# Branch A's queries and keys as two more seven-product quads ahead of the heads, and TensorE's program for the heads written out

## The chip, the core and the metric

The kernel runs on one core of a Trainium2 chip. The metric is the device time of one execution in microseconds (us), the median of several runs. Engines are called TensorE (PE in the rows), VectorE (DVE), ScalarE (ACT) and SyncE (SP); PE and PEld are TensorE's matmuls and its weight loads.

## What is computed

One layer of a decoder trunk for 512 tokens of width 2048, in float32:

```python
h = _rmsnorm(x, norm_g[l])
proj = jnp.einsum('bsd,df->bsf', h, w_in[l])
aq, ak, av, az = parts[0:4]              # branch A: differential attention, 8 heads, each part 1024 wide
b_qkv = parts[4:4 + 3 * n_g]             # branch B: dilated attention, 3 groups of q, k, v, 8 heads
bz = parts[4 + 3 * n_g]
cb, cc, cx, cz = parts[5 + 3 * n_g:9 + 3 * n_g]                         # branch C: short gated convolution
gates = jax.nn.sigmoid(parts[9 + 3 * n_g] + gate_b[l])                  # 3 x 2048 wide
oa = _diff_attention(aq, ak, av, lam, slopes_a)
ya = (_rmsnorm(oa, subln_g[l]) * (1.0 - lam_init)) * jax.nn.silu(az)
x = x + (gates-weighted sum of ya, yb, yc through w_branch_a, _b, _c) @ w_out[l]
```

The change concerns `aq` and `ak`: the part of `h @ w_in` that makes branch A's queries and keys, 2 x 1024 columns.

## The kernel before

Every float32 product is made of three matmuls on operands that are split in a high part (ScalarE copies it, `w_hi`) and a low part (VectorE subtracts, `w_lo`): high times high, high times low, low times high. Weights come in units of 128 x 1024 elements (512 KB). A unit is loaded into a ring of three (`raw`), split into rings of three (`w_hi`, `w_lo`), and used by TensorE. ScalarE may split unit n+3 only when TensorE is done with unit n (`pe_used`), VectorE follows ScalarE (`hi_done`), and TensorE waits for VectorE (`lo_done`).

The program has these stages, each engine with its own list of instructions in written order:

- quad 0 (branch A's values) as plain products, 16 units;
- quads 1 to 3 (branch B's values of the three groups): a quad is 1024 columns for all 512 tokens as a 2 x 2 block product with seven products instead of eight (`quad`, 28 units, 7 x 4 x 2 x 2 x 3 = 336 matmuls of 512 columns). The result has the tokens on the partitions; VectorE scales it by the norm (`take_g`), and ScalarE's queue stores it to `c_dram`;
- the 8 heads. A head has ten blocks of 128 columns, in the order w = 0 to 9: AQ, AK, Q0, K0, Q1, K1, Q2, K2, AZ, BZ (queries and keys of A, of the three groups of B, and the gates of both). A block is 2 units, 48 matmuls of 512 columns (`multiply`), and has the channel on the partitions. VectorE scales a block out of PSUM (`scale_block`), ScalarE and VectorE split AQ, AK, Q0, K0 (`split_block`). Behind each block stand the short steps of attention: for branch A quarter q the scores (`scores_a`), `bias_a` and the maximum, the exponential (`exps_a`), `norm_a`, the transposes on TensorE (`probs_a`) and their split (`turned_a`); for branch B the same with `_b`. Branch A's scores stand at w = 2 to 5, their transposes at w = 3 to 6, its values at w = 7, its square sums (`squares_a`) at w = 8; branch B's four parts start at w = 8 and run to w = 3 of the next head;
- 24 sums of weight blocks for later stages (`sum_units`: 4 additions of 128 x 1024 on VectorE) lie among the heads. The tile `ssum` exists once: it is loaded at step t (a step is one unit), summed behind the split at t + 2, stored behind the split at t + 3, and the next load waits for that store;
- head 0 and head 7 are written out, heads 1 to 6 are a loop of two rounds of three heads, on TensorE, ScalarE and VectorE alike. Head 7 also makes the operands of the quads behind it (`combine_h`);
- quads 4 to 13 (branch C and the gates), the branch products, the output product.

In the first units of quad 4 the rest of head 7's branch B is done.

Of the kernel before, what the change touches and what calls it, by code (L numbers as in the profile page):

```python
# [28 lines left out]
P = 128  # L29
# [5 lines left out]
RING = 3  # L35
NBLK1, NHU1 = 10, 20
# [19 lines left out]


PRODUCTS, STEPS = 7, 28
UNITS_V = 16
QUADS_V, QUADS_C, QUADS_G, QUADS_O = 4, 8, 14, 2  # L60
# [29 lines left out]
SUMS_AT = {0: (5, 10), 1: (0, 5, 10, 15), 2: (0, 5, 10, 15), 3: (0, 5, 10), HEADS - 1: ()}  # L90
SUMS_BEFORE = {0: 0, 1: 2, 2: 6, 3: 10, HEADS - 1: 0}
SUMS_LOOP = 11
# [7 lines left out]
class Head:  # L100
# [4 lines left out]
    def slot(self, t):  # L105
        return (X_H + NHU1 * self.k + t) % RING

    def bank(self, w):
        return (NBLK1 * self.k + w) % RING

    def sums(self, t, at):
        if t - at not in SUMS_AT[self.k]:
            return None
        m = SUMS_BEFORE[self.k] + SUMS_AT[self.k].index(t - at)
        return m if self.j is None else SUMS_LOOP * self.j + m
# [62 lines left out]
SPLIT = [AQ, AK, Q0, K0]  # L178
# [12 lines left out]
def program(nc, wst, wg, ws, x_t, x_tok, cols_d, rows_d, lam_d, const_d, out_d):  # L191
# [8 lines left out]
    with ExitStack() as ctx:  # L200
# [21 lines left out]
        with ExitStack() as c1:  # L222
# [3 lines left out]
            s1("pad0", [P, 2048])  # L226
# [154 lines left out]
        b_saved, b_back = sem("b_saved"), sem("b_back")  # L381
        va_in, vb_in, vg_in, vh_done, vl_done = sem("va_in"), sem("vb_in"), sem("vg_in"), sem("vh_done"), sem("vl_done")
# [212 lines left out]
        def _(pe):  # L595
# [16 lines left out]
            def scaled(i, b):  # L612

                pe.wait_ge(evac_done, NBLK1 * i + (RING + b + 1))

            def split_ready(i, b):

                pe.wait_ge(ql_done, len(SPLIT) * i + (SPLIT.index(b) + 1))

            def scores_a(i, q):  # L620

                n = P * (q + 1)
                split_ready(i, AK)
# [29 lines left out]
            def squares_a(i):  # L653

                pe.wait_ge(sq_split, i + 1)
                pe.wait_ge(s_free, 9 * i + 5)
# [3 lines left out]
            def scores_b(i, c):  # L660

                scaled(i, K2)
                pe.wait_ge(s_free, 9 * i + (6 + c))
# [78 lines left out]
            def blocks(h):  # L742
                i, fresh, last = h.i, h.j is None and h.k == 0, h.j is None and h.k == HEADS - 1
                for w in range(NBLK1):
                    if fresh and w == 0:
                        pe.wait_ge(got, evicted(QUADS_V - 1, 5, 1))
                        pe.wait_ge(b_back, 32)
                    if fresh and w == 2:
                        pe.wait_ge(got, evicted(QUADS_V - 1, 6, 1))
                    pe.wait_ge(evac_done, NBLK1 * i + (w + 1))  # L750
                    pe.wait_ge(lo_done, NHU1 * i + (R_H + 2 * w + 1))
                    multiply(h.bank(w), h.slot(2 * w), act_hi, act_lo, 0, True, False)
                    if w == 8:
                        squares_a(i)
                    if last and w == 9:
                        probs_b(i, 0)
                        scores_b(i, 1)
                    pe.wait_ge(lo_done, NHU1 * i + (R_H + 2 * w + 2))
                    multiply(h.bank(w), h.slot(2 * w + 1), act_hi, act_lo, 8, False, True)
                    if w < 2 and not fresh:  # L760
                        scores_b(i - 1, 2 + w)
                    if w < 3 and not fresh:
                        probs_b(i - 1, 1 + w)
                    if w == 3 and not fresh:
                        values_b(i - 1)
                    if 2 <= w < 6:
                        scores_a(i, w - 2)
                    if 3 <= w < 7:
                        probs_a(i, w - 3)
                    if w == 7:  # L770
                        values_a(i)
                    if w == 8:
                        scores_b(i, 0)
                    if w == 9:
                        if last:
                            scores_b(i, 2)
                        else:
                            scores_b(i, 1)
                            probs_b(i, 0)
# [33 lines left out]
            def free_g(q, p):  # L813
# [3 lines left out]
                if q == QUADS_V and p in (P1, P5, P2):  # L817
                    return {P1: (evac_done, [NBLK1 * HEADS + RING] * 2), P5: (s_free, [9 * HEADS + 1] * 2),
# [11 lines left out]
            def between_g(q, p):  # L830

                def after(u):
# [3 lines left out]
                    if q == QUADS_V:  # L836
                        if n == 1:
                            scores_b(HEADS - 1, 3)
# [122 lines left out]
        def _(act):  # L961
# [45 lines left out]
            def split_1(h, t):  # L1007

                slot = h.slot(t + RING)
                act.wait_ge(raw_in[slot], 16 * h.loads(t + RING))  # L1010
                act.wait_ge(pe_used, NHU1 * h.i + (R_H + t + RING + 1))
                nc.scalar.activation(w_hi[slot][:, :], raw[slot][:, :], ACT.Copy).then_inc(hi_done, 1)  # L1012
# [34 lines left out]
            def split_block(i, w):  # L1047

                act.wait_ge(evac_done, NBLK1 * i + (RING + w + 1))
                nc.scalar.activation(qk_hi[w][:, :], blk[w][:, :], ACT.Copy).then_inc(qh_done, 1)  # L1050

            def tanh_half(i, w):
                act.wait_ge(evac_done, NBLK1 * i + (RING + w + 1))
# [24 lines left out]

            def head(h):
# [16 lines left out]
                for w in range(NBLK1):  # L1096
                    split(2 * w)
                    if last and w == 4:
                        comb_high(5, t1[0], f1, (comb_sum, 5))
                    if last and w == 7:  # L1100
                        comb_high(6, t2[0], f2, (comb_sum, 6))
                    if w in SPLIT:
                        split_block(i, w)
                    if last and w == 9:
                        turned_b(i, 0)
                    split(2 * w + 1)
                    if fresh and w == 1:
                        store_gate(QUADS_V - 1, 2)
                    if w == 3:
# [4 lines left out]
                    if w == 4:  # L1114
                        load_v(i, 1, v_b, vb_in, False)
# [3 lines left out]
                    if w == 5:  # L1119
# [3 lines left out]
                        for g in (1, 2):  # L1123
                            load_v(i, 1 + g, v_g[g], vg_in, True)
                    if w < 3 and not fresh:
                        turned_b(i - 1, 1 + w)
                    if 3 <= w < 7:
                        turned_a(i, w - 3)
                    if w == 9 and not last:
                        turned_b(i, 0)  # L1130
                    if w == 5:
                        act.wait_ge(va_in, 16 * i + 16)
                        high_v(v_a)
                    if w < 2 and not fresh:
                        exps_b(i - 1, 2 + w)
                    if 2 <= w < 6:
                        exps_a(i, w - 2)
                    if w == 7:
                        act.wait_ge(o_free, 2 * i + 2)
                        nc.scalar.activation(sq_a[:, :], o_a[:, :], ACT.Square)  # L1140
                        nc.scalar.activation(sq_hi[:, :], o_a[:, :], ACT.Square).then_inc(sq_ready, 1)
                    if w == 8:
                        act.wait_ge(s_free, 9 * i + 6)
                        nc.scalar.activation(inv_a[:, :], sq_a[:, :], ACT.Sqrt).then_inc(sd_ready, 1)
                    if w == AZ:
                        act.wait_ge(sd_ready, i + 1)
                        tanh_half(i, w)
                    if w in (8, 9):
                        exps_b(i, w - 8)
                    if w == 9:  # L1150
# [3 lines left out]
                    if w == BZ:  # L1154
                        tanh_half(i, w)
# [1101 lines left out]
```

## Time and profile before

| what | us |
|---|---|
| median of 3 runs (2529.17 to 2530.74) | 2530.38 |
| the profiled execution, its own time | 2530.92 |
| its span, first to last instruction | 2529.1 |
| TensorE busy | 2501.1 |
| VectorE busy | 1963.6 |
| ScalarE busy | 1031.8 |

Matmuls overlap in the trace: one of 512 columns is shown with 0.39 us, but the next one starts 0.23 us later, so costs on TensorE are read from starts. A group of rows with the same shape is merged into one row with its count.

### The profile page before, as it was taken

Reading aid. Unit: us, or ns where it says so; the run is one execution under the profiler, and the core shown is the slowest. Engines: PE = TensorE matmul, PEld = TensorE weight load, DVE = VectorE, ACT = ScalarE, POOL = GpSimd, SP = SyncE. Lnnn points to the kernel's source line nnn. Section 1 sums busy time; section 2 is a strip of 40 time slices with the busy share of each in tenths; the row PEclk is TensorE's granted clock in tenths of the full one; section 3 lists DMA queues with packets and bytes.
Section 4 is the critical chain, followed back from the end, with each engine's and each line's share of the span. In section 5 each row is a group of like instructions: output and inputs, shape, how many; then the busy total and the mean of one; then the engine's idle time right before and its main releaser. Section 6 shows DMA issues by size and latency. Waiting matters only on the chain.

```text
span 2529.1 us, 30668 instructions
## 1 busy us (share of the span) xinstructions
PE 2501.1 (99%) x11486; PEld 2065.3 (82%) x11486; DVE 1963.6 (78%) x2294; ACT 1031.8 (41%) x1273; POOL 0.2 (0%) x4
## 2 busy tenths in 40 slices
PE   9999999999999999999999999999999999999998
PEld 8888888888888888888887788888878887788787
DVE  8797746767676767676768887789878897898875
ACT  5343323233333233333244433344444445655644
POOL 0000000000000000000000000000000000000000
PEclk9999999999999999999999999999999999999999
DMA  8255255566665566665235545545566455787665
GB/s 315 96 193 191 78 193 196 187 237 221 237 220 204 188 237 221 237 220 204 81 111 189 211 167 191 174 158 181 186 222 202 165 174 201 275 284 243 216 229 202
DMA packets 172709, 501.98 MB, mean 198 GB/s; under 512 B 13585, under 2 KB 50706, under 8 KB 169362
## 3 DMA queue, kind: packets, MB, share of 16 engines
q1 hardware_dynamic: 88448, 338.44, 38.7%
q10 hardware_dynamic: 84114, 161.56, 18.1%
q8 instruction: 94, 1.54, 0.2%
q14 instruction: 53, 0.43, 0.1%
HBM read 407.67 MB, written 92.27 MB: 198 GB/s over the span
## 4 chain that ended last, share of the span: by engine, by line
PE 89%; DVE 5%; DMA 4%; issue 1%; ACT 1%; ACTq 0%; SPq 0%; DVEq 0%
PE proj L600 14%; PE proj L602 14%; PE proj L601 14%; PE sc_ps L600 6%; PE sc_ps L602 6%; PE sc_ps L601 6%; PE tr_ps L600 5%; PE tr_ps L602 5%; PE tr_ps L601 5%; PE o_ps L600 3%; PE o_ps L602 3%; PE o_ps L601 3%; DVE w_lo L1459 2%; DMA raw<-s_dram 1%; DMA rows<-c_dram 1%; PE tr_ps L637 1%
## 5 line engine op out<-in xcount | busy, mean ns | idle before, releaser
L600 PE MATMUL proj<-act_hi,w_hi 128*128 128x512 f32 x1280 | 505.4, 395 | 1.2 <-DVE w_lo L1503 1.2
L602 PE MATMUL proj<-act_hi,w_lo 128*128 128x512 f32 x1280 | 499.1, 390 | 0.0
L601 PE MATMUL proj<-act_lo,w_hi 128*128 128x512 f32 x1280 | 498.4, 389 | 0.0
L971 ACT ACTIVATE w_hi<-raw 128x1024 fp32r<-128x1024 f32 x280 | 296.9, 1060 | 409.6 <-PE proj L602 127.9
L1459 DVE TENSOR_TENSOR w_lo<-raw,w_hi 128x1024 fp32r<-128x1024 f32 x280 | 341.4, 1222 | 148.5 <-ACT w_hi L971 147.8
L971 ACT ACTIVATE w_hi<-kb 128x1024 fp32r<-128x1024 f32 x240 | 254.4, 1061 | 371.9 <-PE proj L602 133.6
L1459 DVE TENSOR_TENSOR w_lo<-kb,w_hi 128x1024 fp32r<-128x1024 f32 x240 | 293.3, 1223 | 96.3 <-ACT w_hi L971 95.5
L1503 DVE TENSOR_TENSOR w_lo<-raw,w_hi 128x1024 fp32r<-128x1024 f32 x160 | 195.7, 1223 | 128.3 <-ACT w_hi L1012 125.8
L602 PEld LDWEIGHTS proj<-act_hi,w_lo 128*128 128x128 f32 x1280 | 240.3, 188 | 51.1
L600 PEld LDWEIGHTS proj<-act_hi,w_hi 128*128 128x128 f32 x1280 | 240.9, 188 | 49.4 <-DVE w_lo L1503 1.4
L601 PEld LDWEIGHTS proj<-act_lo,w_hi 128*128 128x128 f32 x1280 | 240.6, 188 | 48.0
L1012 ACT ACTIVATE w_hi<-raw 128x1024 fp32r<-128x1024 f32 x160 | 168.3, 1053 | 224.3 <-PE proj L602 219.3
L1036 ACT ACTIVATE sc<-sc,nmax 128x768 f32<-128x768 f32 (+4 forms) x96 | 65.5, 682 | 225.4 <-DVE nmax L1630 126.1
L600 PE MATMUL tr_ps<-w_hi,act_hi 128*128 128x512 f32 x312 | 122.2, 392 | 5.8 <-DVE w_lo L1459 5.7
L600 PE MATMUL sc_ps<-w_hi,act_hi 128*128 128x512 f32 x320 | 125.4, 392 | 0.5 <-DVE w_lo L1459 0.5
L601 PE MATMUL sc_ps<-w_lo,act_hi 128*128 128x512 f32 x320 | 124.5, 389 | 0.0
L600 PE MATMUL sc_ps<-w_hi,tb 128*128 128x512 f32 x312 | 122.1, 391 | 0.0
L602 PE MATMUL sc_ps<-w_hi,tb 128*128 128x512 f32 x312 | 121.5, 389 | 0.0
L601 PE MATMUL sc_ps<-w_lo,tb 128*128 128x512 f32 x312 | 121.4, 389 | 0.0
L601 PE MATMUL tr_ps<-w_lo,act_hi 128*128 128x512 f32 x312 | 121.4, 389 | 0.0
L602 PE MATMUL sc_ps<-w_hi,act_lo 128*128 128x512 f32 x304 | 118.3, 389 | 0.0
L602 PE MATMUL tr_ps<-w_hi,act_lo 128*128 128x512 f32 x288 | 112.1, 389 | 0.0
(318 smaller groups left out, 4551.4 us busy)
## 6 DMA issues: line engine op xcount, KB each, us to landing
raw<-wst SPq DMA_DIRECT2D x160, 512.0 KB, 4.2
raw<-wg SPq DMA_DIRECT2D x112, 512.0 KB, 4.0
kb<-wg SPq DMA_DIRECT2D x24, 2048.0 KB, 8.0
ssum<-ws ACTq DMA_DIRECT2D x24, 2048.0 KB, 9.4
s_dram<-ssum ACTq DMA_DIRECT2D x24, 2048.0 KB, 7.7
raw<-s_dram SPq DMA_DIRECT2D x96, 512.0 KB, 4.3
raw<-ws SPq DMA_DIRECT2D x72, 512.0 KB, 4.3
kb<-wg SPq DMA_DIRECT2D x48, 512.0 KB, 6.8
```

Source lines behind the costliest of these rows:

```text
L600: nc.tensor.matmul(out, w_h, a_h, start=first, stop=False, skip_group_check=shared)
L601: nc.tensor.matmul(out, w_h, a_l, start=False, stop=False, skip_group_check=shared)
L602: return nc.tensor.matmul(out, w_l, a_h, start=False, stop=last, skip_group_check=shared)
L637: end = nc.tensor.transpose(tr_ps[idx % 2][:, n * P:(n + 1) * P], tile, ident[:, :])
L971: nc.scalar.activation(w_hi[r % RING][:, :], src, ACT.Copy).then_inc(hi_done, 1)
L1012: nc.scalar.activation(w_hi[slot][:, :], raw[slot][:, :], ACT.Copy).then_inc(hi_done, 1)
L1036: end = nc.scalar.activation(tile[:, lo:hi], tile[:, lo:hi], ACT.Exp, scale=scale, bias=nmax[:, m:m + 1], accum_out=sums[:, m:m + 1])
L1459: tt(w_lo[r % RING][:, :], src, w_hi[r % RING][:, :].bitcast(f32), ALU.subtract).then_inc(lo_done, 1)
L1503: tt(w_lo[slot][:, :], raw[slot][:, :], w_hi[slot][:, :].bitcast(f32), ALU.subtract).then_inc(lo_done, 1)
```

## The change

- `NHU1` is 16: a head has eight blocks, w = 2 to 9. Branch A's queries and keys are quads 1 and 2, ahead of branch B's values (quads 3 to 5); there are 16 quads instead of 14.
- They lie in `c_dram` with the tokens on the partitions. Per head ScalarE's queue loads the 128 columns of each (`load_qa`), TensorE turns each with four transposes into a PSUM bank (`turn_block`), in the middle of w = 2 (AQ) and w = 3 (AK); ScalarE copies the high part (`high_turn`), VectorE subtracts (`low_turn`).
- The attention steps are spread over the eight blocks: branch A's scores at w = 4 to 7, transposes at w = 5 to 8, values at w = 9, the square sums in the middle of w = 2 of the next head. Branch B runs from w = 8 to w = 5 of the next head.
- The 24 sums stand at other steps (`SUMS_FIRST`, `SUMS_LOOP`), some 4 steps apart; before they were 5 apart or more.
- In head 7 VectorE's long reciprocal (`inverse_a`) goes from w = 9 into unit 6 of the quad behind the heads, the square sums go there too (`squares_last`).
- TensorE's heads 1 to 6 are written out. ScalarE and VectorE keep their loops.

```diff
-NBLK1, NHU1 = 10, 20
+NBLK1, NHU1 = 10, 16
-QUADS_V, QUADS_C, QUADS_G, QUADS_O = 4, 8, 14, 2
+QUADS_V, QUADS_C, QUADS_G, QUADS_O = 6, 10, 16, 2
-SUMS_AT = {0: (5, 10), 1: (0, 5, 10, 15), 2: (0, 5, 10, 15), 3: (0, 5, 10), HEADS - 1: ()}
+SUMS_FIRST = (0, 4, 8, 12)
+SUMS_LOOP = (0, 5, 9, 14, 18, 23, 28, 32, 37, 41)
...
+            def turn_block(h, b):
+                i, bank = h.i, pb[h.bank(b)]
+                pe.wait_ge(qa_in[b], 16 * i + 16)
+                pe.wait_ge(evac_done, NBLK1 * i + (ENTRY[b] + 1))
+                for n in range(4):
+                    end = nc.tensor.transpose(bank[:, n * P:(n + 1) * P], qa[b][:, n, :], ident[:, :])
+                end.then_inc(a_turned, 1)
...
+                    if w == Q0:
+                        if fresh:
+                            pe.wait_ge(got, evicted(QUADS_V - 1, 6, 1))
+                        turn_block(h, AQ)
+                        if not fresh:
+                            squares_a(i - 1)
+                    if w == K0:
+                        turn_block(h, AK)
...
+                    if w < 4 and not fresh:
+                        scores_b(i - 1, w)
+                    if w < 5 and not fresh:
+                        probs_b(i - 1, w - 1)
+                    if w == 5 and not fresh:
+                        values_b(i - 1)
+                    if 4 <= w < 8:
+                        scores_a(i, w - 4)
+                    if 5 <= w < 9:
+                        probs_a(i, w - 5)
...
-            with pe.Fori(0, 2) as j:
-                for k in range(1, 4):
-                    blocks(looped(j, k))
-            blocks(fixed(HEADS - 1))
+            for n in range(1, HEADS):
+                blocks(fixed(n))
...
+            def low_turn(h, b):
+                dve.wait_ge(a_hi, 2 * h.i + (TURNED.index(b) + 1))
+                tt(qk_lo[b][:, :], pb[h.bank(b)][:, :], qk_hi[b][:, :].bitcast(f32), ALU.subtract).then_inc(evac_done, 1)
...
+                    split(t)
+                    if w == Q0:
+                        low_turn(h, AQ)
...
                     if w == 2 and not fresh:
+                        dve.wait_ge(s_ready, 9 * i - 9 + (5 + SQ_AFTER))
+                        ts(sq_a[:, :], sc_ps[0][:, :], 1.0 / P, EPS, ALU.mult, ALU.add).then_inc(s_free, 1)
...
                         if n == 3:
+                            dve.wait_ge(last_sq, 1)
+                            ts(sq_a[:, :], pb[0][:, :], 1.0 / P, EPS, ALU.mult, ALU.add).then_inc(last_read, 1)
                             turned_b(HEADS - 1, 1)
                             norm_b(HEADS - 1, 2)
-                            bias_b(HEADS - 1, 3)
+                            bias_b(HEADS - 1, 3, True)
+                        if n == 6:
+                            inverse_a(HEADS - 1)
```

Three places in VectorE's list. `ssum` rows are a sum of weight blocks, `w_lo` the split of a unit, `nmax` the maximum, `pr` the normalised probabilities that TensorE transposes.

The last quarter of branch A in the loop's first head, before (w = 5 and 6):

```order
L1503 TENSOR_TENSOR w_lo<-raw,w_hi 128x1024
L1626 SCALAR_TENSOR_TENSOR sc<-masks,slope,sc_ps 128x512 x2
...
L1630 TENSOR_SCALAR nmax<-rsum 128x2
...
L1639 SCALAR_TENSOR_TENSOR pr<-sc,rsum,tmp_a 128x512
...
L1503 TENSOR_TENSOR w_lo<-raw,w_hi 128x1024
...
L1495 TENSOR_TENSOR ssum<-ssum 128x1024
```

and now (w = 7 and 8):

```order
L1568 TENSOR_TENSOR w_lo<-raw,w_hi 128x1024
L1559 ISA
L1560 TENSOR_TENSOR ssum<-ssum 128x1024
...
L1563 TENSOR_TENSOR ssum<-ssum 128x1024
L1691 SCALAR_TENSOR_TENSOR sc<-masks,slope,sc_ps 128x512 x2
...
L1695 TENSOR_SCALAR nmax<-rsum 128x2
...
L1704 SCALAR_TENSOR_TENSOR pr<-sc,rsum,tmp_a 128x512
```

The sum stood behind the probabilities and now stands ahead of them; in the loop's first and third head.

The first block of the loop's second head, before (w = 0):

```order
L1658 TENSOR_SCALAR pr<-sc,rsum 128x768
...
L1503 TENSOR_TENSOR w_lo<-raw,w_hi 128x1024
...
L1616 TENSOR_TENSOR stage<-proj,rstd 128x512
```

and now (w = 2):

```order
L1728 TENSOR_SCALAR pr<-sc,rsum 128x768
L1567 ISA
L1568 TENSOR_TENSOR w_lo<-raw,w_hi 128x1024
L1559 ISA
L1560 TENSOR_TENSOR ssum<-ssum 128x1024
...
L1563 TENSOR_TENSOR ssum<-ssum 128x1024
L1708 ISA
L1709 TENSOR_TENSOR qk_lo<-proj,qk_hi 128x512
L1820 ISA
L1821 TENSOR_SCALAR th<-sc_ps 128x512
```

`qk_lo<-proj` is `low_turn`, and `th<-sc_ps` frees the bank that the next scores of branch B need; both stand behind a sum here.

Units 3 to 6 of the quad behind the heads, before:

```order
L1459 TENSOR_TENSOR w_lo<-raw,w_hi 128x1024
L1663 TENSOR_TENSOR pt_lo<-tr_ps,pt_hi 128x4x128
...
L1653 TENSOR_SCALAR nmax<-rsum 128x1
L1459 TENSOR_TENSOR w_lo<-raw,w_hi 128x1024
...
L1658 TENSOR_SCALAR pr<-sc,rsum 128x768
L1459 TENSOR_TENSOR w_lo<-raw,w_hi 128x1024
L1803 TENSOR_SCALAR gin<-proj,rcol 128x512 x2
```

and now:

```order
L1524 TENSOR_TENSOR w_lo<-raw,w_hi 128x1024
L2031 TENSOR_SCALAR th<-proj 128x512
L1733 TENSOR_TENSOR pt_lo<-tr_ps,pt_hi 128x4x128
...
L1723 TENSOR_SCALAR nmax<-rsum 128x1
L1524 TENSOR_TENSOR w_lo<-raw,w_hi 128x1024
...
L1728 TENSOR_SCALAR pr<-sc,rsum 128x768
L1524 TENSOR_TENSOR w_lo<-raw,w_hi 128x1024
L1771 RECIPROCAL tmp_a<-tmp_a 128x512
L1885 TENSOR_SCALAR gin<-proj,rcol 128x512 x2
```

`th<-proj` and the reciprocal have come between the splits.

## Rows read from the trace of the kernel before

**Rows 1.** The page: busy time, share of the span, instructions.

```profile
PE 2501.1 (99%) x11486; PEld 2065.3 (82%) x11486; DVE 1963.6 (78%) x2294; ACT 1031.8 (41%) x1273; POOL 0.2 (0%) x4
```

**Rows 2.** Stretches: us, busy PE, PEld, DVE, ACT, POOL (instructions), clock, DMA share, GB/s.

```profile
622.20:748.42 126.22, 126.22 (x610) 104.71 (x609) 93.60 (x136) 41.83 (x65) 0.00 (x0) 1.00 0.64 229
748.42:876.05 127.63, 126.44 (x609) 104.74 (x608) 89.09 (x132) 41.91 (x65) 0.00 (x0) 1.00 0.54 195
```

**Rows 3.** Waits, one of TensorE's: waited for, us in total, times, longest.

```profile
PE proj L600 <- DVE z_b L1616: 1.6, 1, 1.6
```

**Rows 4.** TensorE in order of time, block matmuls: start, shown duration, line, names, count.

```profile
741.84 0.39 PE L601 MATMUL proj<-act_lo,w_hi 128*128 128x512 f32 x1
...
748.19 0.39 PE L602 MATMUL proj<-act_hi,w_lo 128*128 128x512 f32 x1
```

**Rows 5.** TensorE: four transposes and the first matmul of the next block.

```profile
661.37 0.60 PE L637 MATMUL tr_ps<-ident,pr 128*128 128x128 f32 x4
661.73 0.48 PE L600 MATMUL proj<-act_hi,w_hi 128*128 128x512 f32 x1
```

**Rows 6.** VectorE in order of time: the split of a unit, a sum, what follows.

```profile
626.31 1.23 DVE L1503 TENSOR_TENSOR w_lo<-raw,w_hi 128x1024 fp32r<-128x1024 f32 x1 [1.65 <-ACT w_hi L1012]
627.45 1.22 DVE L1495 TENSOR_TENSOR ssum<-ssum 128x1024 f32<-128x1024 f32 x1
...
632.24 0.68 DVE L1674 TENSOR_TENSOR qk_lo<-stage,qk_hi 128x512 fp32r<-128x512 f32 x1
```

**Rows 7.** VectorE: branch A's last quarter, from bias to probabilities.

```profile
651.52 1.40 DVE L1626 SCALAR_TENSOR_TENSOR sc<-masks,slope,sc_ps 128x512 f32<-128x512 f32 x2
...
655.97 0.17 DVE L1636 RECIPROCAL rsum<-sums 128x2 f32<-128x2 f32 x1 [1.13 <-ACT sc L1036]
...
656.88 0.75 DVE L1639 SCALAR_TENSOR_TENSOR pr<-sc,rsum,tmp_a 128x512 f32<-128x512 f32 x1
```

**Rows 8.** TensorE: the short steps between two blocks (522.96 to 524.16, 698.05 to 699.75).

```profile
522.96 0.50 PE L629 MATMUL sc_ps<-qk_hi 64*128 64x512 f32 x2
...
524.16 0.48 PE L600 MATMUL proj<-act_hi,w_hi 128*128 128x512 f32 x1
...
698.05 0.39 PE L600 MATMUL sc_ps<-qk_hi 128*128 128x512 f32 x1
...
699.75 0.48 PE L600 MATMUL proj<-act_hi,w_hi 128*128 128x512 f32 x1
```

**Rows 9.** TensorE's end of a block, and VectorE's split of the unit it freed.

```profile
812.24 0.39 PE L600 MATMUL sc_ps<-qk_hi 128*128 128x512 f32 x1
...
813.53 1.23 DVE L1503 TENSOR_TENSOR w_lo<-raw,w_hi 128x1024 fp32r<-128x1024 f32 x1 [0.40 <-ACT w_hi L1012]
```

**Rows 10.** Branch B's bias and maximum, an exponential, and the squares' split.

```profile
701.42 0.74 DVE L1646 SCALAR_TENSOR_TENSOR sc<-masks,slope,sc_ps 128x512 f32<-128x512 f32 x1
...
703.71 0.15 DVE L1653 TENSOR_SCALAR nmax<-rsum 128x1 f32<-128x1 f32 x1
...
1323.63 0.92 ACT L1036 ACTIVATE sc<-sc,nmax 128x768 f32<-128x768 f32 x1
...
1309.62 0.69 DVE L1776 TENSOR_TENSOR sq_lo<-th,sq_hi 128x512 fp32r<-128x512 f32 x1 [1.22 <-ACT sq_hi L1141]
```

**Rows 11.** Head 7's end and the quad behind it, VectorE, TensorE and ScalarE.

```profile
1321.14 0.63 ACT L1144 ACTIVATE tmp_a<-th 128x512 f32<-128x512 f32 x1
...
1331.59 3.34 DVE L1701 RECIPROCAL tmp_a<-tmp_a 128x512 f32<-128x512 f32 x1
...
1335.81 0.47 PE L600 MATMUL proj<-w_hi,act_hi 128*128 128x512 f32 x1 [1.63 <-DVE z_b L1616]
...
1347.97 1.22 DVE L1459 TENSOR_TENSOR w_lo<-raw,w_hi 128x1024 fp32r<-128x1024 f32 x1
...
1349.29 0.47 PE L600 MATMUL sc_ps<-w_hi,tb 128*128 128x512 f32 x1
```

**Rows 12.** Transfers into and out of `ssum`, 48 of them.

```profile
DMA to landing us min/median/max: 7.4/8.8/11.3
```

More of the change, by code:

```diff
@@ L175, in gated, with step_b @@
     return 8 * q + 2 * GATED.index(d) + s + 1
-SPLIT = [AQ, AK, Q0, K0]
+SPLIT = [Q0, K0]
+TURNED = [AQ, AK]
+SQ_AFTER = 2
+def step_b(c, last):
+    return 5 + c + (not last and c >= SQ_AFTER)
 TURN_P = [4, 6, 8, 10]
@@ L743, in blocks @@
                 i, fresh, last = h.i, h.j is None and h.k == 0, h.j is None and h.k == HEADS - 1
-                for w in range(NBLK1):
-                    if fresh and w == 0:
-                        pe.wait_ge(got, evicted(QUADS_V - 1, 5, 1))
+                for w in range(Q0, NBLK1):
+                    t = 2 * (w - Q0)
+                    if fresh and w == Q0:
                         pe.wait_ge(b_back, 32)
[L748 to L752, printed above, removed]
-                    if w == 8:
[L754 to L773, printed above, removed]
@@ new lines, in blocks @@
+                    if last and w == 9:
+                        values_a(i)
+                        probs_b(i, 0)
+                        scores_b(i, 1, True)
+                    pe.wait_ge(lo_done, NHU1 * i + (R_H + t + 2))
+                    multiply(h.bank(w), h.slot(t + 1), act_hi, act_lo, 8, False, True)
+                    if w < 4 and not fresh:
[4 more added lines that the diff above has]
+                        values_b(i - 1)
@@ L1113, in head @@
                         load_v(i, 0, v_a, va_in, False)
-                    if w == 4:
-                        load_v(i, 1, v_b, vb_in, False)
+                        if not last:
+                            load_qa(i + 1)
+                    if w == 6:
+                        load_v(i, Q_V, v_b, vb_in, False)
                         if not fresh:
@@ L1123, in head @@
                         for g in (1, 2):
[L1124 to L1128, printed above, removed]
+                            load_v(i, Q_V + g, v_g[g], vg_in, True)
+                    if w < 5 and not fresh:
+                        turned_b(i - 1, w - 1)
+                    if 5 <= w < 9:
+                        turned_a(i, w - 5)
@@ L1142, in head @@
-                    if w == 8:
-                        act.wait_ge(s_free, 9 * i + 6)
-                        nc.scalar.activation(inv_a[:, :], sq_a[:, :], ACT.Sqrt).then_inc(sd_ready, 1)
+                    if w == 3 and not fresh:
+                        act.wait_ge(vb_in, 16 * i)
+                        act.wait_ge(o_ready, 2 * i - 1)
+                        high_v(v_b)
+                    if w < 4 and not fresh:
+                        exps_b(i - 1, w)
+                    if w == 3:
+                        for b in SPLIT:
+                            split_block(i, b)
@@ L1149, in head @@
                         exps_b(i, w - 8)
-                    if w == 9:
+                    if last and w == 9:
                         act.wait_ge(vb_in, 16 * i + 16)
@@ L1229, in _ @@
                     end_of(q, n)
+                    if q == QUADS_V - 1 and n == 16:
+                        for m in range(8):
+                            act.wait_ge(g_stored[m], 16 * Q_V)
+                        load_qa(0)
                     if q == QUADS_V - 1 and n == 23:
@@ L1708, in join_a, with copy_o, low_squares @@
                 stt(y_a[:, :], o_a[:, :], 0.5, blk[AZ][:, :], ALU.mult, ALU.mult).then_inc(y_ready, 1)
+            def copy_o(i):
+                dve.wait_ge(o_ready, 2 * i + 1)
+                nc.vector.tensor_copy(o_a[:, :], o_ps[:, :]).then_inc(o_free, 1)
+            def low_squares(i):
+                dve.wait_ge(sq_ready, i + 1)
+                tt(sq_lo[:, :], sq_a[:, :], sq_hi[:, :].bitcast(f32), ALU.subtract).then_inc(sq_split, 1)
             def head(h):
@@ L1722, in head @@
                 link(nc.vector.tensor_copy(slope[:, 0:1], slopes[:, bass.ds(4 * i, 1)]))
-                for w in range(NBLK1):
-                    if w < 3 and not fresh:
-                        norm_b(i - 1, 1 + w)
-                    if fresh and w == 3:
+                for w in range(Q0, NBLK1):
+                    t = 2 * (w - Q0)
+                    if w < 5 and not fresh:
+                        norm_b(i - 1, w - 1)
+                    if fresh and w == 5:
                         for n in range(8):
                             dve.wait_ge(g_stored[n], 16 * QUADS_V)
-                    if 3 <= w < 7:
-                        norm_a(i, w - 3)
+                    if 5 <= w < 9:
+                        norm_a(i, w - 5)
                     if w == 9:
                         norm_b(i, 0)
-                    split(2 * w)
+                    split(t)
+                    if w == Q0:
+                        low_turn(h, AQ)
+                    if w == K0:
+                        low_turn(h, AK)
                     if last:
```

212 lines of the change are left out of this document (119 added, 93 removed).

## The prediction

> **What bounds the kernel now.** I read the page's busy times first: TensorE is busy 2501.1 of 2529.1 us [rows 1]; some 28 us idle is all that better waiting could give, and anything else must come from fewer or shorter matmuls. Then the heads, head by head: from one head to the next TensorE takes 126.22 us and is busy throughout, at a granted clock of 1.00 (the 2.4 GHz level), while VectorE is busy 93.60 of it [rows 2]. The round that holds the loop's jump takes 127.63 us, 1.41 more. TensorE's own waits come last: near the heads there is one of note, 1.6 us at the end of head 7 [rows 3]. So the heads run at TensorE's pace, and VectorE, at 74%, is the engine that could take over.
>
> **Matmuls taken out and put in.** From 741.84 to 748.19 lie 28 steps of block matmuls, 0.2267 us each [rows 4]. Out: 8 heads x 2 blocks x 48 = 768 matmuls, 174.1 us. In: 2 quads x 336 = 672, 152.3 us. The quads in place show no gaps to speak of, and a quad's own VectorE work is the same in all of them, so I take the same pace for the two new ones. Net -21.8 us.
>
> **Transposes.** Four take 0.36 us from first start to the next block's matmul, and that matmul shows 0.48 instead of 0.39 because the switch delays it [rows 5]: 0.45 us a turn, 16 turns, 7.2 us. But the short steps now form eight groups behind blocks instead of ten, which spares two such switches a head, about 1.7 us in all. Net +5.5. The bounds: 4 (every switch hidden) and 10 (0.60 shown per group). The Trainium skill, "TensorE: Matmul & The Clock Gate", Part 4: PE-mode transpose, gives about 275 ns for one transpose in a kernel; by that the 64 would cost 17.6 us. The rows decide against it: four start within 0.36 us, so the shown duration is latency that overlaps.
>
> **The loop.** TensorE's one jump back costs 1.41 us [rows 2]; written out it goes: -1.4. VectorE's and ScalarE's loops stay, and their jumps are covered as now, since the first thing that TensorE needs of them in a head comes several us later.
>
> So far: -21.8 + 5.5 - 1.4 = -17.7 us, if nobody waits. A head then takes 105 us; VectorE loses four splits and two scalings, some 6 us, so it is busy about 87 of 105, 83%. An average doesn't tell whether TensorE waits; the places where a sum of weight blocks stands ahead of something urgent do. A split with a sum behind it holds VectorE 5.93 us (626.31 to 632.24) [rows 6], and a split starts 1.29 us after TensorE has freed the unit [rows 9].
>
> **Wait 1, the last quarter's probabilities.** In the loop's first and third head a sum stands in w = 7 between the split and `bias_a(3)`. Counted from TensorE's end of that block: split and sum done at 1.29 + 5.93 = 7.2; bias, maximum and exponential 4.45 more (651.52 to 655.97); `pr` written 1.66 after that (to 656.88 + 0.75) [rows 7]: 13.3. TensorE wants it after the scores and transposes behind w = 7 (1.20, 522.96 to 524.16) [rows 8] and one block of 48 with its switch (11.0): 12.2. It waits 1.1 to 1.2, in heads 1, 3, 4 and 6: +4.8. Now the sum stands behind `pr`, which is why no such wait exists.
>
> **Wait 2, the start of heads 2 and 5.** A sum stands behind the first split of w = 2. From TensorE's end of the first half: 1.29 + 5.93, then `low_turn` 0.6, then the scaling of the square sums 0.7 (the size of the 0.68 row) [rows 6]: 8.6. TensorE meanwhile has the turn 0.36, two square matmuls 0.6 and 24 matmuls 5.4: 6.4. It then wants the bank for `scores_b(2)`: +2.2, twice, +4.4. Behind this VectorE has slack again.
>
> **Wait 3, the squares after heads 0, 2 and 5.** Their last block has a sum behind its first half. From TensorE's end of the head, T: VectorE has split and summed at T - 5.5 + 7.2 = 1.8, then gate, scaling, split and copy (0.8 + 0.6 + 1.1 + 0.6): 4.9; bias and maximum 2.4 (701.42 to 703.71 + 0.15): 7.35; ScalarE's exponential 1.1 and two squares 1.2, VectorE's split 0.7 [rows 10]: 10.3. TensorE: values (12 matmuls, 3840 columns, 1.7 to 1.9), scores and transposes 1.70 (698.05 to 699.75) [rows 8], half a block 5.6, the turn 0.4: 9.5. +0.8 three times, +2.5. Without that sum it is 8.7 against 9.5, no wait.
>
> **The quad behind the heads.** Now TensorE starts it at 1335.81, having waited for VectorE's scaling behind the 3.34 us reciprocal; the `w_lo` for its fifth unit is ready at 1349.19, and TensorE takes it at 1349.29 [rows 11]: there is 0.1 us of slack. Added ahead of that split: `low_squares` 0.6, the square sums' scaling 0.6, and ScalarE's root (0.63) in front of the transposes' copy, 2.1 us in all, against 0.5 of new square matmuls on TensorE: a wait of 1.5. Before unit 7 the reciprocal adds its 3.4, of which some 1 us is slack left by then: 2.4. Together +3.9. In head 7 itself `inverse_a` goes, but a `comb_low` and `copy_o` come ahead of BZ's scaling: I get 1.9 us of waits there for 2.3 now, -0.4.
>
> **Sum.** -17.7 + 4.8 + 4.4 + 2.5 + 3.9 - 0.4 = -2.5 us. The profiled execution (2530.92, its span 2529.1) stands 0.5 above the median; as a difference it applies to the median alike: 2530.4 - 2.5 = 2527.9, say 2528.
>
> **Rivals.**
> (a) VectorE's slack takes it all. If waits 1 to 3 don't appear the time is -17.7 + 3.5 = -14.2: 2516; if those of the quad don't either, 2513. For it: each wait is a difference of two sums of five to eight terms, and 1 us on either side cancels most of them; the ring gives TensorE two units of margin everywhere else. Against: the terms are rows, and the order puts 4.8 us of sums ahead of each.
> (b) Slower: the one `ssum` tile. Sums 4 steps apart leave, by my count from the store at step 8 to the sum at step 11, 18.3 us for a store and a load; the median landing is 8.8 each, the largest 11.3 [rows 12]. With medians it fits by 0.7. With the largest it is 4.3 us late, and VectorE, in order, holds the split and wait 1 grows by as much in four heads: +17, 2545. It decides from 1.9 us late in each (+7.5). Against it: DMA is 64% busy now [rows 2] and hardly more later.
> (c) Slower by more of the kind I count: the same differences come out 1 us larger at nine places, 2537.
> (d) The written-out program gives nothing, because jump and fetching were not the cost: +1.4, within my range. The heads written out now, 0 and 7, show no fetch stall.
>
> **How the numbers follow.** A measurement of this kernel can tell about 0.2%, 5.1 us, from no change. My case, a total between -5 and +5, 0.50, with 2528 as the likeliest; (a), wholly or by half, 0.34; (b) and (c) 0.16. (d) lies in the first. The range takes in half of (a) and the near part of (c): 2517 to 2536; my case alone spans 2525.4 to 2535.4.
>
> **What would show it.** Head to head 105 us where nothing waits; in the loop's first and third head a wait of TensorE's transposes for `pr` of about 1.2; in heads 2 and 5 a wait of TensorE's scores for `th` of about 2; waits for `sq_lo` of about 0.8 in three heads; no gap at the former jump; in the quad behind the heads two waits for `w_lo`, 1.5 and 2.4. VectorE waiting for the load of `ssum` would be (b). If TensorE's waits between the quads and quad 6 add up to under 7 us, (a) is right. If the two new quads take other than 76.2 us each, or a turn other than 0.45, the first part is wrong.

## The result

The changed kernel takes 2536.57 us (median of 20 runs, 2532.20 to 2539.59) where the kernel before takes 2529.45 in the same comparison: 1.0026 times as long, with an interval of 1.0020 to 1.0032. A second comparison gave 1.0028 (1.0018 to 1.0039). That is 5 to 7 us slower (the medians of the two comparisons are 7.1 and 4.8 apart, the means 6.1 and 5.4), where 2.5 us faster was forecast. The time lies just outside the range. The profiled execution took 2532.20 us, with a span of 2530.4.

The page of the changed kernel, busy times, against [rows 1]: TensorE 9 us less, VectorE 74 us more.

```profile
PE 2491.8 (98%) x11454; PEld 2055.6 (81%) x11454; DVE 2037.6 (81%) x2362; ACT 1061.5 (42%) x1297; POOL 0.2 (0%) x4
```

TensorE's waits in the changed kernel (waited for, us in total, times, longest):

```profile
PE sc_ps L617 <- DVE w_lo L1524: 9.4, 8, 2.3
PE sc_ps L617 <- DVE th L1821: 4.3, 2, 2.1
PE tr_ps L659 <- DVE pr L1704: 3.8, 4, 1.0
PE sc_ps L679 <- DVE sq_lo L1786: 2.3, 3, 1.3
...
PE sc_ps L617 <- issue: 1.5, 1, 1.5
```

The three waits forecast in the heads are all there, in the number forecast: two for `th`, four for `pr`, three for `sq_lo`. The last line is the first wait of the quad behind the heads, at 1349.05: the profile names no engine that ended it. Now the stretches: the heads, then all behind them, of the changed kernel and then of the kernel before (us, busy PE, PEld, DVE, ACT, POOL, clock, DMA share, GB/s).

```profile
479.86:1333.45 853.59, 842.00 (x4107) 695.33 (x4105) 661.92 (x980) 301.55 (x479) 0.00 (x0) 1.00 0.63 218
1333.45:2530.40 1196.95, 1172.02 (x5223) 963.37 (x5223) 988.22 (x1011) 563.37 (x621) 0.00 (x0) 1.00 0.60 204
```

```profile
327.89:1335.81 1007.92, 1004.07 (x4813) 831.20 (x4811) 716.14 (x1031) 336.40 (x517) 0.00 (x0) 1.00 0.56 198
1335.81:2529.10 1193.29, 1171.15 (x5221) 963.02 (x5221) 982.79 (x1008) 558.54 (x615) 0.00 (x0) 1.00 0.60 205
```

Up to the heads the change adds 479.86 - 327.89 = 152.0 us (forecast 152.3), in the heads it takes 154.3 off, and behind them it adds 3.7. The forecast for the heads was -158.7 (-174.1 + 5.5 - 1.4 + 4.8 + 4.4 + 2.5 - 0.4). The larger part of the 4.4 that is missing there stands behind the two waits for `th`. TensorE around the first one (start, shown duration, line, names, count, idle before):

```profile
697.04 0.39 PE L619 MATMUL proj<-act_hi,w_lo 128*128 128x512 f32 x1
699.56 0.65 PE L617 MATMUL sc_ps<-qk_hi 128*128 128x512 f32 x1 [2.13 <-DVE th L1821]
700.02 0.63 PE L618 MATMUL sc_ps<-qk_lo,qk_hi 128*128 128x512 f32 x1
700.44 0.63 PE L619 MATMUL sc_ps<-qk_hi,qk_lo 128*128 128x512 f32 x1
```

and TensorE's stretches there (us, busy, granted clock, DMA share, GB/s):

```profile
690.00:696.00 6.00, 6.00 (x30) 1.00 0.22 59
696.00:700.00 4.00, 1.87 (x8) 0.96 0.32 130
700.00:704.00 4.00, 4.00 (x18) 0.61 1.04 390
704.00:710.00 6.00, 6.00 (x30) 1.00 0.37 119
```

After the wait the matmuls are 0.42 to 0.46 apart instead of 0.2267, and the granted clock is below 1.00: for some 3.4 us it is 0.50, the 1.2 GHz level. The eight us from 699.56 on lose 1.7 us by it, and the same follows the wait at 1022.76. In the profile of the kernel before the clock is below 1.00 in the last 10 us alone. The prediction has no such term.

### The profile page after: what moved, and what is told of

Its sections match the earlier page's. It is cut to its first block, busy times and chain, and to the rows that moved or that the text cites. A ratio compares the mean times of both kernels' runs of the same rounds, so it can differ in the third digit from the quotient of the medians.

```text
span 2530.4 us, 30366 instructions
## 1 busy us (share of the span) xinstructions
PE 2491.8 (98%) x11454; PEld 2055.6 (81%) x11454; DVE 2037.6 (81%) x2362; ACT 1061.5 (42%) x1297; POOL 0.2 (0%) x4
## 4 chain that ended last, share of the span: by engine, by line
PE 83%; DVE 8%; DMA 5%; issue 2%; ACT 2%; ACTq 0%; DVEq 0%; SPq 0%
PE proj L617 11%; PE proj L619 11%; PE proj L618 11%; PE tr_ps L617 6%; PE tr_ps L619 6%; PE tr_ps L618 6%; PE sc_ps L617 6%; PE sc_ps L618 6%; PE sc_ps L619 6%; PE o_ps L618 3%; PE o_ps L619 3%; PE o_ps L617 3%; DVE w_lo L1524 2%; DMA rows<-c_dram 1%; PE tr_ps L659 1%
## 5 line engine op out<-in xcount | busy, mean ns | idle before, releaser
L1003 ACT ACTIVATE w_hi<-kb 128x1024 fp32r<-128x1024 f32 x280 | 297.3, 1062 | 436.2 <-PE proj L619 154.4
L1524 DVE TENSOR_TENSOR w_lo<-kb,w_hi 128x1024 fp32r<-128x1024 f32 x280 | 342.9, 1225 | 116.8 <-ACT w_hi L1003 116.2
L617 PE MATMUL proj<-act_hi,w_hi 128*128 128x512 f32 x1024 | 406.4, 397 | 0.0
L619 PE MATMUL proj<-act_hi,w_lo 128*128 128x512 f32 x1024 | 399.7, 390 | 0.0
L618 PE MATMUL proj<-act_lo,w_hi 128*128 128x512 f32 x1024 | 399.1, 390 | 0.0
L619 PEld LDWEIGHTS proj<-act_hi,w_lo 128*128 128x128 f32 x1024 | 192.5, 188 | 41.4
L617 PEld LDWEIGHTS proj<-act_hi,w_hi 128*128 128x128 f32 x1024 | 193.2, 189 | 38.3
L618 PEld LDWEIGHTS proj<-act_lo,w_hi 128*128 128x128 f32 x1024 | 192.9, 188 | 38.4
L617 PE MATMUL tr_ps<-w_hi,tb 128*128 128x512 f32 x328 | 128.4, 392 | 0.4 <-DVE w_lo L1524 0.4
L619 PE MATMUL tr_ps<-w_hi,tb 128*128 128x512 f32 x328 | 127.7, 389 | 0.0
L618 PE MATMUL tr_ps<-w_lo,tb 128*128 128x512 f32 x328 | 127.6, 389 | 0.0
```

What stands on the lines that cost most here:

```text
L617: nc.tensor.matmul(out, w_h, a_h, start=first, stop=False, skip_group_check=shared)
L618: nc.tensor.matmul(out, w_h, a_l, start=False, stop=False, skip_group_check=shared)
L619: return nc.tensor.matmul(out, w_l, a_h, start=False, stop=last, skip_group_check=shared)
L1003: nc.scalar.activation(w_hi[r % RING][:, :], src, ACT.Copy).then_inc(hi_done, 1)
L1524: tt(w_lo[r % RING][:, :], src, w_hi[r % RING][:, :].bitcast(f32), ALU.subtract).then_inc(lo_done, 1)
```

## The experiments

Each kernel's own median says less than its difference to the kernel before run beside it. Of every run the mean granted clock is recorded too, to three decimals, and I give its mean over the executions of a kernel: a mean clock that is 0.001 lower is 2.5 us of TensorE's time lost in 2530.

**The changed kernel again**, no edit.

> The changed kernel unedited, for a second profile of it and as the partner of the three others. Its profiled execution took 2532.2 us where the median of 20 was 2536.6; the profiled one had a mean granted clock of 0.998, most others 0.996 to 0.997. Theory (clock): this profile shows, beside the two stretches at a granted clock of 0.50 behind the 2.13 us waits for the squares' mean in heads 2 and 5, further such stretches behind waits of about 2 us, and its span is longer by half of their length. Rival (waits): waits of TensorE are longer or more in it, with the clock as it was. Rival (pitch): matmuls apart from waits are further apart. Time 2536, and 1.0026 times the kernel before.

Measured: 2536.94, 1.0028 (1.0018 to 1.0039). Its profile has the same two waits, 2.13 us each, but behind the first, at 699.72, the clock stays up:

```profile
696.00:700.00 4.00, 1.87 (x9) 1.00 0.33 134
700.00:704.00 4.00, 4.00 (x24) 1.00 1.02 394
```

and it stays up behind the second. It falls instead behind a wait of 2.08 us in the quad behind the heads (1357.2) and behind one of 2.55 at 2095. So the low clock is no fixed part of the `th` waits: one wait of about 2 us is followed by it in one execution and not in the next. Nor do busy DMA queues decide it: their share behind the wait is 1.04 where the clock fell and 1.02 where it stayed. The mean clock of the executions is 0.9984 for the kernel before (25 of them) and 0.9969 to 0.9970 for the changed one (8 and 20): 3.6 us of difference or a little more. The later waits for `w_lo` vary between executions as well (at 2095 to 2097, 2.32 in one profile and 2.55 in the other; one of 2.02 at 2154 in the second alone).

**The sum at the first step of heads 2 and 5 behind the scaling.**

```diff
 def split(t):
-    m = h.sums(t, SUM_AT)
-    if m is not None:
-        sum_units(m)
+    if t:
+        sums_at(t)
...
 if w == 2 and not fresh:
     dve.wait_ge(s_ready, 9 * i - 9 + (5 + SQ_AFTER))
     ts(sq_a[:, :], sc_ps[0][:, :], 1.0 / P, EPS, ALU.mult, ALU.add).then_inc(s_free, 1)
+    sums_at(0)
```

> Only the sum of the weights' parts that VectorE does at the first step of heads 2 and 5 is moved, from ahead of the low part of the turned queries and the scaling of the squares' mean to behind both. Theory (clock): the two 2.13 us waits of TensorE go (4.3 us), and with them the stretches at a granted clock of 0.50 behind them (3.3 us in the profile): 7.5 us less than the changed kernel, 2529, with a mean clock of 0.999 and less spread between executions. Rival (waits only): the waits go and the clock stays as it is, 4.3 us less, 2532. Rival (the wait moves): the scaling of the next block's bank comes as late as before and TensorE waits there; 0 to 2 us less.

Measured: 2531.06, 0.9994 (0.9985 to 1.0003) of the kernel before, and 5.9 us less than the changed kernel run beside it (2536.94). VectorE at head 2's start (the low part, the turn's low part, the scaling, then the sum):

```profile
694.43 1.23 DVE L1568 TENSOR_TENSOR w_lo<-raw,w_hi 128x1024 fp32r<-128x1024 f32 x1 [0.96 <-ACT w_hi L1044]
695.57 0.68 DVE L1709 TENSOR_TENSOR qk_lo<-proj,qk_hi 128x512 fp32r<-128x512 f32 x1
696.17 0.68 DVE L1825 TENSOR_SCALAR th<-sc_ps 128x512 f32<-128x512 f32 x1
696.77 1.22 DVE L1560 TENSOR_TENSOR ssum<-ssum 128x1024 f32<-128x1024 f32 x1
```

The `th` waits are gone from the profile (4.3 us) and nothing takes their place: the wait came from the order on VectorE, not from its load. The mean clock rises from 0.9969 to 0.9976, about 1.7 us, so the two parts make 6.0, where the medians differ by 5.9 and the means by 7.4. "Waits only" (4.3) falls short of both, but with 8 and 11 executions of the two kernels, which spread by 11 and 7 us, this run alone doesn't settle it; the pauses below do.

**All sums in the loop moved**: the edit above, and one line.

```diff
-SUMS_LOOP = (0, 5, 9, 14, 18, 23, 28, 32, 37, 41)
+SUMS_LOOP = (0, 5, 10, 14, 18, 22, 26, 32, 37, 42)
```

> All sums inside the loop of VectorE stand where no step that TensorE soon waits for is behind them: the one at the first step behind the scaling, those at units 11, 9 and 14 of a head at 12 and 8, and one at 12. Theory (clock): the waits of 2.13 (2), 0.96 (4) and 1.35 (2 of the 3, head 0's stays) go, and the low clock behind the first two: 4.3 + 3.8 + 1.7 + 3.3 = 13 us less than the changed kernel in its profile (2519), and 15 or more in the medians (2521). Rival (waits only): 9.8 us less, 2526.5. Rival (the sums have to be somewhere): VectorE's sum at unit 12 makes the step behind it late and half of the gain is lost, 2530.

Measured: 2523.47, 0.9969 (0.9960 to 0.9978); run again later, beside other kernels:

> The moved sums alone once more, beside the version that also orders the quad behind the heads. 0.997 times the kernel before, as the first time, with a mean clock of 0.9976.

2523.27, 0.9968 (0.9956 to 0.9979). So 8 us less than the kernel before and 13.5 less than the changed one. Of the waits for `th`, `pr` and `sq_lo` one is left, head 0's:

```profile
PE sc_ps L679 <- DVE sq_lo L1786: 1.6, 1, 1.6
```

The heads take 839.7 us in both profiles, 168.2 less than before, and from one head to the next TensorE takes 105.37 us six times over (forecast 105). Without head 0's wait of 1.6 us the heads are at 838.1, against 837.5 for the forecast without waits 1 to 3 (1007.92 - 174.1 + 5.5 - 1.4 - 0.4). The mean clock is 0.9976 and 0.9979, hardly better than with one sum moved: it falls in these two profiles behind waits at 1346, 2021, 2087 and 2085, outside the heads.

**The `th` waits made longer.**

```diff
+if t == 0:
+    for n in range(2):
+        link(nc.vector.tensor_copy(masks[:, 0:1024], masks[:, 0:1024]))
 sum_units(m)
```

> Ahead of the sum at the first step of heads 2 and 5 VectorE does two more copies of a constant tile onto itself, 1.2 us each, so the two waits of TensorE there grow from 2.13 to about 4.5 us. Theory (clock): 4.8 us for the waits themselves, and the stretch at 0.50 behind each stays at 3.3 us or grows, and comes in every execution: 2537 in the profile, 2541 to 2543 in the median. Rival (waits only): 4.8 us, with the low clock no longer tied to these places. Rival (slack): the copies are taken up and less than 2 us shows.

Measured: 2543.46, 1.0050 (1.0034 to 1.0065), 6.5 us more than the changed kernel. The copies were shorter than I took them to be: the waits are 3.69 us each, 7.4 together, 3.1 more than before. Most of the other 3.4 is, by the mean clock of these four executions, the clock: it falls from 0.9969 to 0.9958, 2.8 us, and in the profile it is low behind both (eight us from each wait's end on):

```profile
701.36:709.36 8.00, 8.00 (x29) 0.67 0.85 307
1026.96:1034.96 8.00, 8.00 (x33) 0.79 0.85 309
```

**Pauses of chosen length.** The kernel with the moved sums, and twelve waits of TensorE for GpSimd, two of a length in each of heads 1 to 6. GpSimd starts when TensorE is done with a block's last unit.

```diff
+for n, size in enumerate(PAUSES):
+    i, w = n // len(PAUSE_W) + 1, PAUSE_W[n % len(PAUSE_W)]
+    pool.wait_ge(pe_used, NHU1 * i + (R_H + 2 * (w - Q0) + 2 + RING))
+    for m, part in enumerate(size):
...
+        nc.gpsimd.memset(pad[:, 0:part], 0.0).then_inc(paused, 1)
```

> To see the clock after waits of a chosen length, the kernel with the moved sums (heads with one wait over 0.5 us, head 0's) gets twelve pauses: twice in each of heads 1 to 6, after the second part of the fifth and of the eighth block, TensorE waits for GpSimd, which zeroes an unused tile once (128, 512, then 1024 columns), twice, three and four times. Heads 1 to 6 have pauses of one length each, growing from head to head, from under 1 us to some 4 us or more. Theory (clock): no stretch at a granted clock of 0.50 behind the pauses under about 1.9 us, one behind most of those over it. Rival (the clock falls without regard to waits): the stretches stand anywhere in the heads. Rival (it needs much longer pauses): none in the heads.

Measured: 2553.62, 1.0092 (1.0062 to 1.0121). The waits, one of each length:

```profile
617.05 0.33 PE L660 MATMUL tr_ps<-ident,pr 128*128 128x128 f32 x1 [0.32 <-POOL pad L1003]
...
723.64 0.33 PE L660 MATMUL tr_ps<-ident,pr 128*128 128x128 f32 x1 [0.65 <-POOL pad L1003]
...
830.98 0.44 PE L660 MATMUL tr_ps<-ident,pr 128*128 128x128 f32 x2 [1.07 <-POOL pad L1003]
...
939.75 0.79 PE L660 MATMUL tr_ps<-ident,pr 128*128 128x128 f32 x3 [2.08 <-POOL pad L1003]
...
1053.65 0.69 PE L660 MATMUL tr_ps<-ident,pr 128*128 128x128 f32 x2 [3.09 <-POOL pad L1003]
...
1170.69 0.69 PE L660 MATMUL tr_ps<-ident,pr 128*128 128x128 f32 x2 [4.10 <-POOL pad L1003]
```

and the eight us behind each of them (us, busy, instructions, granted clock, DMA share, GB/s):

```profile
617.03:625.03 8.00, 7.98 (x42) 1.00 0.86 326
723.60:731.60 8.00, 7.96 (x41) 1.00 0.72 249
831.05:839.05 8.00, 8.00 (x42) 1.00 1.00 361
939.75:947.75 8.00, 8.00 (x35) 0.79 1.00 375
...
1053.65:1061.65 8.00, 8.00 (x30) 0.64 1.03 333
...
1170.69:1178.69 8.00, 8.00 (x32) 0.70 1.08 375
```

The clock is low behind all six pauses of 2.08 us and more, and behind none of the six up to 1.07. The heads grow from 839.7 to 874.9: 35.2 us. The pauses are 22.6 of that (two each of 0.32, 0.65, 1.07, 2.08, 3.09 and 4.10), and the clock's loss behind the six long ones is 12.1 (8 us times what is missing to 1.00). The two make 34.7: a wait costs its length, and where the clock falls it costs 1.7 to 2.9 more. The lengths grow with time here, so the place could be the cause instead; but both profiles without pauses show 1.00 throughout the heads. And the DMA share, 1.00 behind the pause of 1.07 and 1.00 behind that of 2.08, doesn't tell them apart.

Over all twelve profiles of this study, waits of TensorE by length, and how many had a low clock in the eight us behind them: 0.9 to 1.7 us, none of 83; 1.7 to 2.0, 6 of 33; 2.0 to 2.2, 10 of 17; over 2.2, 14 of 17. The longest without it is the 3.12 us wait at 2094 in the first profile of the kernel before, the shortest with it 1.79. The Trainium skill, "TensorE: Matmul & The Clock Gate", section "HAM oscillation", describes this fall for short bursts of matmuls between transfer waits of about 3 to 5 us, after which the next burst starts at the lower level. These traces agree that work behind such a wait starts at the lower level, but show it from waits of 1.8 to 2.1 us on.

**The loop alone**, on the kernel before.

```diff
-with pe.Fori(0, 2) as j:
-    for k in range(1, 4):
-        blocks(looped(j, k))
-blocks(fixed(HEADS - 1))
+for n in range(1, HEADS):
+    blocks(fixed(n))
```

> The kernel before with one edit of the change alone: TensorE's program for the heads written out, without a loop. Forecast: 1.4 us less than the kernel before, the one turn of the loop in which TensorE stood still. Rival: it gives nothing, since the stretch behind the turn waits for VectorE by as much. Rival: the longer program costs TensorE instruction fetches at many places, 1 us or more longer. Its profile also shows a second time how long the stages behind the heads take with the code of before (1185 us from the quad behind the heads to the last matmul in the first profile, 1189 to 1197 in five profiles of kernels with the change): theory, 1186 to 1192, since most of that spread is between executions; rival, 1185 again, and the change costs 4 to 12 us there.

Measured: 2532.51, 1.0004 (0.9995 to 1.0013). In the profile the heads take 1006.51 us against 1007.92, 1.41 less, as forecast; this can't be told in the whole time. In the profile of the kernel before the jump's cost stands as 1.19 us of idle at 827.39 that is put down to `w_lo`; with the code written out, and VectorE's loop kept, it is gone. TensorE's stretches from the heads to the end:

```profile
327.85:1334.36 1006.51, 1003.85 (x4813) 1.00 0.56 198
1334.36:2530.30 1195.94, 1172.24 (x5221) 1.00 0.59 204
```

Behind the heads, with code that is the same, this execution takes 1195.94 where the first took 1193.29: a single profile says nothing of 3 us there.

**The quad behind the heads, reordered twice.** First the low part of unit 4 ahead of head 7's last biases and the reciprocal at step 10; by itself, and with the moved sums.

```diff
 if n == 3:
     ...
     norm_b(HEADS - 1, 2)
+    lo_g(q, 4)
     bias_b(HEADS - 1, 3, True)
-if n == 6:
+if n == 10:
     inverse_a(HEADS - 1)
```

> The changed kernel with two moves in the quad behind the heads, on VectorE alone: the low part of unit 4 stands ahead of the last biases of head 7, and the reciprocal of branch A's roots (3.35 us) stands at step 10 instead of 6. Theory (waits plus clock): the waits of 1.47 and 2.07 us in this quad go, and with them the low clock that followed the second in four of the five profiles so far (1.6 us each): 4 to 5 us less than the changed kernel, 2531.5 to 2532.5. Rival (the reciprocal only moves the wait): at step 10 it is ahead of a low part and of the combination that the third product needs, and a wait of 1 to 2 us comes back near 45 us into the quad: 1.5 to 3 us less. Rival (the quad was as long before): the quad behind the heads gains nothing against the kernel before.

> The moved sums and the two moves in the quad behind the heads together. Theory: the gains add, 13.5 us of the moved sums in the medians and 4 to 5 of the quad, so 2518 to 2519, 0.995 times the kernel before. Rival (the clock falls elsewhere as often): with fewer waits of about 2 us left the mean clock stays at 0.9976 and 2521 comes out. Rival (not additive): the quad's waits return because the sums leave other work behind, 2523.

Measured: 2536.92, 1.0020 (1.0011 to 1.0029), and 2525.8, 0.9976 (0.9964 to 0.9988) with the sums. Neither gains on the kernel that it starts from. The waits of 1.47 and 2.07 became the first two of these three; the third was there already (1.36 at 1392.37 in the changed kernel, 1.43 at 1390.30 in the kernel before):

```profile
1350.63 0.50 PE L617 MATMUL sc_ps<-w_hi,tb 128*128 128x512 f32 x1 [1.91 <-DVE w_lo L1524]
...
1373.05 0.50 PE L617 MATMUL proj<-w_hi,tb 128*128 128x512 f32 x1 [1.83 <-DVE w_lo L1524]
...
1392.82 0.50 PE L617 MATMUL proj<-w_hi,act_hi 128*128 128x512 f32 x1 [1.52 <-DVE w_lo L1524]
```

ScalarE shows where the first comes from: the high part of unit 5 stands behind the exponentials, and these wait for the biases that the edit made later.

```profile
1346.82 0.94 ACT L1068 ACTIVATE sc<-sc,nmax 128x768 f32<-128x768 f32 x1 [3.05 <-DVE nmax L1723]
...
1348.28 1.04 ACT L1003 ACTIVATE w_hi<-raw 128x1024 fp32r<-128x1024 f32 x1
```

The second comes with the reciprocal, as the rival had it. So I moved that high part ahead of the exponentials too, and cut the reciprocal in halves at steps 6 and 10:

> The moved sums, and the quad behind the heads in another order than the last attempt: on VectorE the low part of unit 4 ahead of head 7's last biases, on ScalarE the high part of unit 5 ahead of head 7's last exponentials (it had come behind them, and TensorE waited 1.9 us for it), and the reciprocal of 3.35 us in two halves, at steps 6 and 10. Theory: the waits of 1.44 and 2.09 us become less than 1 us together, no low clock follows there, and nothing as long as 1.8 us comes at step 11: 4 to 5 us less than with the moved sums alone, 2519 to 2520. Rival (VectorE is full for 40 us there): as in the last attempt the waits come back 20 us later, and the time stays within 2 us of the moved sums alone.

Measured: 2522.31, 0.9966 (0.9954 to 0.9978), beside 2523.27 for the moved sums alone. In this quad the moved sums alone have waits of 1.46, 2.11 and 1.35 us, the last at 1378.6; this version has 1.05 and 1.68, the last at 1377.3. The profile's last matmul comes 2.5 us earlier; the medians differ by 1 us, which this comparison can't tell from nothing. It is the fastest of the kernels, but not shown to beat the moved sums.

## Why the prediction was wrong

By its own steps:

- **Matmuls, transposes, loop**: right. The two quads took 152.0 us (152.3). With the sums moved the heads come out within 0.6 us of what these terms make of them, in part because two small waits shrank by more than the -0.4 forecast: in head 7 from 1.9 us of idle to 1.2, and in head 0 from 0.7 to none. The jump's 1.41 us is gone in both written-out programs.
- **Wait 1** (`pr`, forecast four of 1.2): four, 0.96 idle and 1.11 over the usual pitch (667.83 to 669.17, less 0.23): 4.4 for 4.8.
- **Wait 2** (`th`, two of 2.2): two, 2.29 over the pitch: 4.6 for 4.4. That the sum's place makes it is shown by moving the sum.
- **Wait 3** (`sq_lo`, three of 0.85): three, 2.3 us of idle in all, 1.35 of it after head 0, where VectorE had also waited 0.8 us for the tile of the sum: 2.3 for 2.5. That the total fits is partly luck: the other two are 0.47 and 0.46, about half of the forecast, and the one after head 0 is 1.20 to 2.06 in the ten profiles that have it.
- **The quad behind the heads** (1.5 and 2.4, 3.9 in all): two new waits, 1.47 and 2.07, at the units named. The 2.1 us that the prediction puts ahead of the first don't come out of its own terms (0.6 + 0.6 + 0.63 is 1.8), so its 1.5 should have been 1.2. Until the matmuls with `v_g` it is 4.5 us longer than before, and 0.9 more is lost by the next landmark, the transposes 356 us in.
- **Rivals.** (a), VectorE's slack takes the waits, is wrong. (b), the sum's tile late: wrong where it was priced, and seen only in head 0; its transfers land in 9.6 and 7.5 us in the median, and the sum in front of the `pr` waits starts without waiting for them. (c), more of the same kind, is not what happened either: the waits were of the size forecast. (d), the written-out program gives nothing, is wrong in the heads (1.41 us less) and too small to tell in the total.

**The step that failed** is the price of a wait. The sum took every wait at its own length, with TensorE at the 2.4 GHz level throughout, because [rows 2] show 1.00 and the kernel before has nothing longer than 1.63 us near the heads. The change puts three waits of 2.07 to 2.13 us there. In the first profile two of them are followed by the 1.2 GHz level, 1.7 us each. The account of that profile then closes: -2.5, +3.4 for the clock, +1.0 for what else the heads took more than forecast (-154.3 - 3.4 = -157.7 for -158.7), +0.6 and +0.9 for the quad and the stretch behind it, -0.3 ahead of the heads, and -1.7 behind the 356th microsecond of the quad, where this execution waited less than the one of before: +1.4, for 1.3 measured. Nor was the 1.00 of [rows 2] the whole picture: the profile that they come from has a mean clock of 0.999, and the kernel's executions 0.9984, so the clock falls at times in the kernel before too.

The comparisons show 5 to 7 us. The executions' mean clocks say 3.6 us (0.9984 against 0.9970) for the clock's part, and the other terms are nearly the same in both profiles of the changed kernel: -2.5 + 3.6 + 1.0 + 0.6 + 0.9 - 0.3 = 3.3. The 0.9 is no sure part of the change: from the matmuls with `v_g` to the transposes it takes 331.7 and 330.4 us with the changed kernel and 330.9 and 331.7 with the code of before. Of the miss of 7 to 10 us (-2.5 forecast, 5 to 7 measured) the clock is thus the largest term that the runs show, not the whole. Some 2 to 5 us stay open, which can be as much as the clock's part, and the profiles don't hold them. From those `v_g` matmuls to the last matmul, less what the clock lost, it is 1158.9 and 1160.6 us with the changed kernel, 1159.8 and 1160.7 with the code of before. And both profiled executions of the changed kernel are on the short side of its runs (2532.2 and 2534.2, medians 2536.6 and 2536.9). The candidates are the waits for `w_lo` from 1790 on, which differ between executions: 1.46 to 1.80 near 2030 in all twelve profiles, 2.3 to 3.1 near 2095 in eleven and 1.23 in one, others of up to 2.0 in some. Whether the change has a further part in them these runs don't settle.

With the clock in the sum the forecast would have been 2531 to 2532, and the range some 4 us higher, with "slower" as likely as "faster". It was too narrow for the same reason: it had no term for something that a wait of about 2 us sets off or not.

The second thing that the prediction had in its hands and didn't use: it named a sum ahead of an urgent step as the cause of eleven to twelve us of waits, and its own count shows VectorE with 18 of 105 us free in a head. The waits were not VectorE's load. Moved by a step or two, the same work fits, and the change is worth 8 us.

## What to carry to other kernels

Where an engine that sets the pace starts to wait, add to each wait of about 2 us or more what the clock does behind it: here 1.7 us, in about half of the cases at 2.0 to 2.2 us, in most above that, and in none of 83 from 0.9 to 1.7. When a change shortens a stage, look in the slower engine's list for long deferrable work (here sums of 4.8 us) that stands ahead of a step with a deadline; move that before judging the change. And moving one instruction on one engine moves the queue of the next that waits for it: the low part put ahead of the biases made ScalarE's split of unit 5 0.9 us later in the quad, and the wait came back there.

## What was not expected of the hardware

- After a wait of TensorE of 1.8 to 4.1 us the granted clock can be 0.50 for some 3.4 us, and up to 5.7, with TensorE busy throughout, and then is 1.00 again. The same place in the same kernel shows it in one execution and not in another (waits of 2.13 at 699.56 and 699.72).
- It goes with a large part of the difference between executions of one kernel: the changed kernel's 20 executions have mean clocks of 0.996 to 0.998, and their times rise from 2533.9 us (mean of the five at 0.998) to 2537.6 (the five at 0.996).
- GpSimd zeroes 1024 float32 columns in 0.96 us, which gives TensorE 1.07 us of idle time: a cheap way to make a wait of chosen length.
